# Mixer attention: a third order of the score blocks, and two matmuls instead of three for the sums over later keys

## What is computed

```
log_weight[j, query] = z[j] - sum over keys j' >= j (and before the query) of f[j']
weight = exp(min(log_weight, 0)) where key < query, else 0
output = weights @ values
```

## Time and profile before

| | |
|---|---|
| median of 3 executions | 837.95 us |
| the profiled execution | 838.62 us, span 836.8 us |
| TensorE busy | 825.9 us, 99% of the span |
| VectorE, ScalarE, GpSimd busy | 620.4, 505.2, 125.3 us |
| granted TensorE clock, mean | 0.998 |

### The profile page before, as it was taken

How to read it: one execution, slowest core, us unless ns; L and a number is a source line. 1 busy time by engine, 2 the same in 40 slices (tenths; PEclk the granted TensorE clock), 3 DMA queues, 4 the chain that set the end, 5 groups by cost and what they waited for, 6 DMA issues and landing times.

```text
span 836.8 us, 16974 instructions
## 1 busy us (share of the span) xinstructions
PE 825.9 (99%) x6832; PEld 799.0 (95%) x6832; DVE 620.4 (74%) x1047; ACT 505.2 (60%) x879; POOL 125.3 (15%) x120
## 2 busy tenths in 40 slices
PE   8999999999999999999999999999999999999997
PEld 8999999999999999999999999999998999888896
DVE  6647888886666689777664478999899696568765
ACT  6446566555444576555554368787968554356755
POOL 1000000000000305443441100043515010000002
PEclk9999999999999999999999999999999999999999
DMA  8754435345665536655666635646545375554331
GB/s 308 263 166 134 152 106 172 127 146 182 181 190 185 171 102 205 200 181 183 194 190 192 188 95 165 192 140 188 178 140 175 106 234 188 180 176 128 127 101 51
DMA packets 39853, 139.81 MB, mean 167 GB/s; under 512 B 4432, under 2 KB 5088, under 8 KB 39648
## 3 DMA queue, kind: packets, MB, share of 16 engines
q1 hardware_dynamic: 38160, 135.90, 51.0%
q10 hardware_dynamic: 1616, 2.84, 1.1%
HBM read 137.65 MB, written 1.06 MB: 166 GB/s over the span
## 4 chain that ended last, share of the span: by engine, by line
PE 83%; DVE 12%; ACT 2%; POOL 1%; issue 1%; DMA 1%; DVEq 0%; SPq 0%; ACTq 0%; POOLq 0%
PE ps L1844 63%; PE ps L1909 4%; DVE weights_lo L1100 4%; PE ps L1868 4%; PE ps L1847 4%; DVE arena L1411 1%; PE ps L2029 1%; PE ps L2055 1%; DVE arena L1420 1%; PE ps L2317 1%; PE ps L2335 1%; ACT weights_hi L557 1%; PE ps L1965 1%; PE ps L2325 1%; DMA raw_weights<-weights_in 1%
## 5 line engine op out<-in xcount | busy, mean ns | idle before, releaser
L1100 DVE TENSOR_TENSOR weights_lo<-raw_weights,weights_hi 128x1024 fp32r<-128x1024 f32 x251 | 311.9, 1247 | 83.3 <-ACT weights_hi L557 82.1
L557 ACT ACTIVATE weights_hi<-raw_weights 128x1024 fp32r<-128x1024 f32 x250 | 262.2, 1053 | 132.4 <-PE ps L1844 55.4
L1844 PE MATMUL ps<-x_hi,weights_hi 128*128 128x256 f32 (+3 forms) x1184 | 341.6, 289 | 0.3 <-DVE arena L1475 0.2
L1844 PE MATMUL ps<-x_lo,weights_hi 128*128 128x256 f32 (+3 forms) x1184 | 333.8, 282 | 0.0
L1844 PE MATMUL ps<-x_hi,weights_lo 128*128 128x256 f32 (+3 forms) x1184 | 333.1, 281 | 0.0
L1844 PEld LDWEIGHTS ps<-x_hi,weights_hi 128*128 128x128 f32 x1184 | 222.8, 188 | 6.7 <-issue 5.6
L1844 PEld LDWEIGHTS ps<-x_lo,weights_hi 128*128 128x128 f32 x1184 | 222.9, 188 | 0.7 <-issue 0.5
L1844 PEld LDWEIGHTS ps<-x_hi,weights_lo 128*128 128x128 f32 x1184 | 223.2, 189 | 0.0
L1844 PE MATMUL ps<-y_lo,weights_hi 128*128 128x256 f32 (+1 forms) x488 | 137.4, 282 | 0.0
L1844 PE MATMUL ps<-y_hi,weights_hi 128*128 128x256 f32 (+1 forms) x488 | 137.2, 281 | 0.0
L1844 PE MATMUL ps<-y_hi,weights_lo 128*128 128x256 f32 (+1 forms) x488 | 137.1, 281 | 0.0
(11 more groups left out here) (288 smaller groups left out, 1184.2 us busy)
## 6 DMA issues: line engine op xcount, KB each, us to landing
raw_weights<-weights_in SPq DMA_DIRECT2D x251, 512.0 KB, 3.7
arena<-decay_rows ACTq DMA_DIRECT2D x8, 256.0 KB, 4.0
masks<-masks_in SPq DMA_DIRECT2D x1, 1186.0 KB, 8.3
raw_weights<-weights_in SPq DMA_DIRECT2D x4, 256.0 KB, 5.3
hidden<-xT_in SPq DMA_DIRECT2D x3, 272.0 KB, 5.8
hidden<-xT_in SPq DMA_DIRECT2D x1, 276.0 KB, 3.1
gate_w<-gate_w_in ACTq DMA_DIRECT2D x1, 256.0 KB, 5.7
out<-arena ACTq DMA_DIRECT2D x1, 256.0 KB, 2.1
```

The costliest lines, as they stand in the source:

```text
L557: a.sig(A(whi[:, s * CW:(s + 1) * CW], raw[:, (c % RAW) * CW:(c % RAW + 1) * CW], ACT.Copy), "hi_ready")
L1100: d.sig(TT(wlo[:, s * CW:(s + 1) * CW], raw[:, (c % RAW) * CW:(c % RAW + 1) * CW], whi[:, s * CW:(s + 1) * CW].bitcast(F32), ALU.subtract) ...
L1844: ins = mm(bank(BANK_OF[no])[:, 0:b - a], wt, x_[:, kt, a:b], start=s0, stop=s1)
```

## The change

The blocks are laid out in another order and cut otherwise: key block 0 with all queries (columns 0 to 257), key block 1 with queries 256 to 271 (258 to 273), key block 1 with queries 128 to 255 (274 to 401), and key block 2 with queries 240 to 271 (402 to 433). Queries 240 to 255 of key block 2 lie before its keys, so that these 16 columns are masked; their place in f holds the sum of key blocks 1 and 2. ZC becomes 434, and the f buffer has the same 434 columns. `scores` makes products of 258, 128, 32 and 16 columns, `attend` of 258, 128, 16 and 16 (it skips the masked columns). `survive` makes one matmul of 434 columns and one of 160 for each part and head. In `fail` one instruction of 2 x 434 columns takes the place of two, of 2 x 144 and 2 x 274, and the mask goes over 2 x 2 x 160 in place of 2 x 2 x 144. The mask table grows by 32 columns.

```diff
-LATE = T - 128
-Z1, Z0, ZE = TAIL, TAIL + LATE, TAIL + 2 * LATE
-ZC = ZE + 128 - TA
-PIECES = ((Z0, 0, 128, T), (Z1, 1, 128, T), (ZE, 0, TA, 128), (0, 2, 256, T))
-FG = TAIL + 128
-FC = ZC + TAIL
-EDGE = FC - FG
+Z1A, Z1B, Z2 = NA, NA + TAIL, NA + TAIL + P
+ZC = Z2 + 2 * TAIL
+PIECES = ((0, 0, TA, T), (Z1B, 1, 128, 256), (Z2, 2, 256 - TAIL, T), (Z1A, 1, 256, T))
...
-                for c0, c1, at in ((0, FG, 0), (FG, ZC, FG + TAIL)):
-                    d.step(STT(out=fz[:, :, at:at + c1 - c0], in0=z[:, :, c0:c1], scalar=0.0, in1=sp[:, :, c0:c1],
-                               op0=ALU.max, op1=ALU.add))
+                d.step(STT(out=fz[:, :, 0:ZC], in0=z[:, :, 0:ZC], scalar=0.0, in1=sp[:, :, 0:ZC],
+                           op0=ALU.max, op1=ALU.add))
...
-                d.sig(TT(fz[:, :, FG:FG + TAIL], fz[:, :, 0:TAIL], fz[:, :, FG + TAIL:FG + 2 * TAIL], ALU.add),
+                d.sig(TT(fz[:, :, Z2:Z2 + TAIL], fz[:, :, Z2 + TAIL:ZC], fz[:, :, Z1A:Z1B], ALU.add),
                       "f_ready")
...
-                        mm(zb[:, FG:ZC], at_or_later, f_[:, FG + TAIL:FC], start=False, stop=False,
-                           skip_group_check=True)
-                        mm(zb[:, 0:FG], at_or_later, f_[:, 0:FG], start=False, stop=False, skip_group_check=True)
-                        ins = mm(zb[:, FG:ZE], later, f_[:, 0:FG + TAIL], start=False, stop=n == 1,
+                        mm(zb[:, 0:ZC], at_or_later, f_, start=False, stop=False, skip_group_check=True)
+                        ins = mm(zb[:, 128 - TA:Z1B], later, f_[:, Z1B:Z2 + 2 * TAIL], start=False, stop=n == 1,
                                  skip_group_check=True)
...
                 for n, (c0, k, t0, t1) in enumerate(PIECES):
+                    if k == 2:
+                        c0, t0 = c0 + TAIL, t0 + TAIL
```

More of the change, by code:

```diff
@@ L209, in build @@
         spare = MERGED * KT * NA
-        f_hi, f_lo = v3(yhi_t[:, spare:spare + 2 * FC], 2), v3(ylo_t[:, spare:spare + 2 * FC], 2)
-        later = yhi_t[:, spare + 2 * FC:spare + 2 * FC + P]
-        at_or_later = yhi_t[:, spare + 2 * FC + P:spare + 2 * FC + 2 * P]
+        f_hi, f_lo = v3(yhi_t[:, spare:spare + 2 * ZC], 2), v3(ylo_t[:, spare:spare + 2 * ZC], 2)
+        later = yhi_t[:, spare + 2 * ZC:spare + 2 * ZC + P]
+        at_or_later = yhi_t[:, spare + 2 * ZC + P:spare + 2 * ZC + 2 * P]
         osq_hi, osq_lo = yhi_t[:, 16 * L:16 * L + 512], ylo_t[:, 16 * L:16 * L + 512]
@@ L246, in build @@
         sp = A1(2, ZC)
-        fz = A1(2, 2 * EDGE)
+        fz = A1(2, 2 * Z1B)
         aw = A1(2, ZC)
@@ L642, in fail_high @@
                 for e in range(2):
-                    a.sig(A(f_hi[:, e, :], fz[:, e, 0:FC], ACT.Copy), "f_hi")
+                    a.sig(A(f_hi[:, e, :], fz[:, e, 0:ZC], ACT.Copy), "f_hi")
             def softplus_part(p):
@@ L1172, in fail @@
                 d.settle()
-                for c0, c1, at in ((0, FG, 0), (FG, ZC, FG + TAIL)):
-                    d.step(STT(out=fz[:, :, at:at + c1 - c0], in0=z[:, :, c0:c1], scalar=0.0, in1=sp[:, :, c0:c1],
-                               op0=ALU.max, op1=ALU.add))
+                d.step(STT(out=fz[:, :, 0:ZC], in0=z[:, :, 0:ZC], scalar=0.0, in1=sp[:, :, 0:ZC],
+                           op0=ALU.max, op1=ALU.add))
                 d.settle()
-                edges = fz.rearrange("p e (s c) -> p e s c", s=2)[:, :, :, 0:FG]
+                edges = fz.rearrange("p e (s c) -> p e s c", s=2)[:, :, :, 0:ZC - Z1B]
                 o = MASKS["stick"][0]
-                keep = msk[:, o:o + 2 * (ZC - FG)].rearrange("p (s c) -> p s c", s=2)[:, :, 0:FG]
-                d.step(TT(edges, edges, keep.unsqueeze(1).to_broadcast([P, 2, 2, FG]), ALU.mult))
+                keep = msk[:, o:o + 2 * Z1B].rearrange("p (s c) -> p s c", s=2)[:, :, 0:ZC - Z1B]
+                d.step(TT(edges, edges, keep.unsqueeze(1).to_broadcast([P, 2, 2, ZC - Z1B]), ALU.mult))
                 d.settle()
-                d.sig(TT(fz[:, :, FG:FG + TAIL], fz[:, :, 0:TAIL], fz[:, :, FG + TAIL:FG + 2 * TAIL], ALU.add),
+                d.sig(TT(fz[:, :, Z2:Z2 + TAIL], fz[:, :, Z2 + TAIL:ZC], fz[:, :, Z1A:Z1B], ALU.add),
                       "f_ready")
@@ L1194, in fail_low @@
                     dve.wait_ge(S("f_hi"), 2 * p + e + 1)
-                    d.sig(TT(f_lo[:, e, :], fz[:, e, 0:FC], f_hi[:, e, :].bitcast(F32), ALU.subtract), "f_lo")
+                    d.sig(TT(f_lo[:, e, :], fz[:, e, 0:ZC], f_hi[:, e, :].bitcast(F32), ALU.subtract), "f_lo")
             def att_low(p):
```

## The result

The changed kernel takes 839.21 us in the median of 17 executions (838.73 to 840.03), the kernel before 837.95 (17 executions on the same chips, 837.58 to 838.97). The ratio is 1.0015, 95% interval 1.0008 to 1.0021: slower, by 0.7 to 1.8 us; the ratio itself is under the 0.2% that I had set as the bound of "no change", and the upper end of its interval lies at it. Forecast were 838.7 us, with 836.9 to 839.8 as the range. The profiled execution took 838.92 us, with a span of 837.1.

The account below looks back on a forecast made before the run. The prediction took TensorE's own work to bound the mixer's loop. Over eight steps `survive` -1.3, `scores` +1.4 and `attend` +0.65 made +0.7 us on 837.95, so 838.7 us, range 836.9 to 839.8.

Parts of the forecast that it names:

- `survive`, -0.17 us: Mixer step, 12 matmuls become 8: the stretch goes from 1.36 to 1.19 us, 0.17 less.
- `scores`, +0.17: Mixer step, same count of passes, other widths: `scores` goes from 1.04 to 1.21 us, 0.17 more.
- The rule of the larger of stream and next load: TensorE: from one pass to the next takes its streaming or the next weight load (112 ns in `scores`), whichever is longer.
- `attend`, +0.08: Mixer step, same columns cut otherwise: `attend` goes from 0.91 to 0.99 us, 0.08 more.
- ScalarE, VectorE and the mask table at nothing: Wider instructions (ScalarE 0.14 us a step, VectorE 0.16) and 0.1 us of mask transfer are hidden, so cost nothing.
- 1.0 us is left: Mixer: of the 1.29 us from `log_weight`'s end to `scores`' start, 1.0 us of slack remains after the change.
- Rival 3: Mixer: `log_weight` ends too late for `scores` if VectorE loses over 1.0 us a step; 840.3 us, chance 0.07.
- The sum, +0.7 us: Eight mixer steps: `survive` -1.3, `scores` +1.4, `attend` +0.65, together +0.7 us, 838.7 on the median.
- my own case: The prediction's main case, chance 0.72: 838.0 to 839.4 us, from the bounds of wide matmul and narrow passes.
- Rival 1: Mixer: columns alone count and no load shows; +0.45 us in all, 838.4 us, chance 0.08.
- Rival 2: Mixer: the gain of `survive` comes, the losses in `scores` and `attend` don't; -1.1 us, 836.9 us, chance 0.08.
- Rival 4: `scores`: the two heads' 258-column products don't run side by side; +3.5 us, 842.2 us, chance 0.02.

Follow-up runs that it names:

- e2: Kernel before with only the change's `survive`, matmuls of 434 and 160 columns in place of 274, 144 and 160: 836.79 us against 838.07.
- e3: Changed kernel with `survive` again in three matmuls, of 274, 160 and 160 columns: 840.49 us.
- e4: Changed kernel with the same blocks in the opposite order, narrow first, in `scores` and `attend`: 840.10 us.
- e6: Changed kernel with `scores` in three products (258, 144, 32 columns), from a second copy of the queries written by VectorE: 837.69 us.
- e10: Changed kernel with each Abs on ScalarE done twice, the second waiting for the first: 843.07 us.
- e7: Changed kernel with `scores` and `attend` both in three products, by query copies on VectorE and weight copies on ScalarE: 839.05 us.
- e8: Changed kernel with `scores` and `attend` both in three products, both copies made by GpSimd: 837.39 us against 838.01 of before.
- e1: Kernel before with only 32 more columns in the mask table: 837.79 us against 838.07.
- e13: Changed kernel with the one `fail` instruction in two again (2 x 144, 2 x 290 columns): 838.91 us, ratio 1.0008.

## Why the prediction was right, point by point

- *TensorE is the bound in the mixer, and its own work is what counts.* Right: it has no wait from 60 to 195 us before or after, and e2 and e3 turn a step's 0.160 and 0.166 us into 1.3 us each (838.07 to 836.79, 839.21 to 840.49).
- *`survive`, -0.17 us.* Right: -0.173 in the change, -0.161 in e2. The wide matmul at 0.197 us and the load at 0.113 are 0.310 a pair; the loads show 0.31.
- *`scores`, +0.17.* Right: +0.168. The rule of the larger of stream and next load gave 1.21 (1.210), 1.31 for e4 (1.306) and 1.02 for e6 (1.022).
- *`attend`, +0.08.* Right: +0.084.
- *ScalarE, VectorE and the mask table at nothing.* Right for the change's steps, by less cover than I put. The step of the prediction that failed is "1.0 us is left", read as the distance from `log_weight` to `scores` in one step of a loop that TensorE sets. That is the slack behind one wait. What counts when a delay comes back every step is the period of the chain that closes on itself: 14.9 us (e10) against 15.31, 0.4 us. Rival 3 is real with that number, and e7 is its case: 0.5 us more in the chain, a shorter step on TensorE, and the whole gain was gone.
- *The sum, +0.7 us.* The mixer has +0.75. The term that was missing is the +0.31 in a stage that the diff doesn't touch: both make 1.06 of the measured 1.26 (0.7 to 1.8). I had charged one instruction fewer on VectorE as a small saving; its side effect, later instructions that move to other places of the stream, is a loss. That 839.21 still lies between the 838.0 and 839.4 of my own case is in part luck: those bounds were set for the wide matmul and the narrow passes, which came out as priced, and what used them up was another term.
- *Rival 1, columns alone:* `scores` would have grown by 27 ns, and it grew by 168; `survive` by 29, and it fell by 173. The formula of the Trainium skill's "TensorE: Matmul & The Clock Gate", section "Back-to-back issue gap", gives the same 27 ns as an estimate, and the traces don't agree. The prediction set it against its own rule too sharply: the section calls the formula the gap of isolated matmuls and says that at few columns it counts too little, since it leaves out the weight loads.
- *Rival 2*, no loss in `scores` and `attend`: out by 168 and 84 ns. *Rival 4*: the 258-column products of the two heads do run side by side (2 x 0.218 in the sum that gives 1.210).

## What to carry to other kernels

Count matmuls by the larger of their own stream and the next one's weight load, in order, and merge narrow ones only where no new narrow one is left over: the change took four uncovered loads out of `survive` and put two more into `scores` and two shorter ones into `attend`. Before other engines get more work per step, add up the chain that leads from a wait back to itself in the next step, and compare this period with the bound's; the gap behind a single wait overstates it (1.0 against 0.4 us here). A copy that makes narrow operands contiguous can pay if an idle engine makes it: the same two copies cost the whole gain on VectorE and ScalarE (e7, 1.0014) and left a little of it on GpSimd (e8, 0.9990).

## What I had not expected of the hardware

- Eight VectorE instructions fewer, some 400 us earlier in the kernel, cost 0.3 us: five other kernels with the shorter stream have it too (0.22 to 0.32), and seven traces with the old count or more (before twice, e1, e2, e6, e7, e13, from -0.17 to 0.00) don't. VectorE has some 0.35 us of idle time at records 447, 703, 831 and 959 of its stream where nothing else covers it, 128 or a multiple of it apart.
- Where these two instructions of VectorE and GpSimd meet, the order in which they start decides which one is long. A 128 x 1024 `split_lo` takes 1.22 us and GpSimd's 128 x 256 addition 1.67 if VectorE is first, 1.61 and 0.73 if GpSimd is.
- A 128-column load in the halves of the array's rows costs 112 ns for both heads together, the 64-column loads of `attend` 54; with these two numbers the parts of the kernels here come out within some 10 ns.
